# A hybrid encoder layer on one core: another order of the projections in the heads phase

## The reference

```
h = rms_norm(x, norm_mix);  u, q, zf, zb, iv, g = split(h @ w_in)          # six parts of 512
k = (1-lb) * sigmoid(-z);  f = 1-k                                         # forward (zf) and backward (zb)
o = gated recurrence of (silu(q), k, iv, f), forward + backward, 4 heads of 128
y_rec = rms_norm(o, hgrn_out_norm) * silu(g)                               # over the 128 values of a head
y_fourier = per-group product with w_fnet of real(fft2(u))
x = x + concat(y_fourier, y_rec) @ w_out
x = x + expert_choice_ffn(rms_norm(x, norm_ffn))                           # 16 experts, top-k tokens of each
return rms_norm(x, norm_final)
```

## Time and profile before

| | before |
|---|---|
| time, median of 3 | 3081.16 us (3079.77 to 3086.99) |
| span of the profiled execution | 3080.7 us |
| TensorE busy (matmul) | 2841.2 us, 92% |
| VectorE busy | 1684.3 us, 55% |
| ScalarE busy | 1352.7 us, 44% |
| GpSimd busy | 225.1 us, 7% |
| heads phase | from 52.8 us, its last matmul near 728 us, the next phase's loads from 731.1 us |

### The profile page before, as it was taken

One profiled execution on the slowest core, in us unless ns is written; L12 is line 12 of the kernel. 1 busy time (PEld: TensorE's weight loads), 2 busy tenths in 40 slices (PEclk: granted clock), 3 DMA queues, 4 the chain that ended last, 5 costly groups with the idle time before them and its releaser, 6 DMA issues. The chain is left out here.

```text
span 3080.7 us, 33698 instructions
## 1 busy us (share of the span) xinstructions
PE 2841.2 (92%) x13072; PEld 2310.5 (75%) x13072; DVE 1684.3 (55%) x1861; ACT 1352.7 (44%) x1324; POOL 225.1 (7%) x258
## 2 busy tenths in 40 slices
PE   6998989898899399999999999999999999999992
PEld 5777777787677377777877877877778778778771
DVE  4455555543233755655655566556556555665562
ACT  5233333322243245454554555554545545545442
POOL 2010101010100110000000000000000000000001
PEclk9999999999999599999999999999999999999996
DMA  4000000004732456565665665665656656656645
GB/s 133 14 18 28 18 28 18 28 31 144 242 127 89 154 201 218 219 237 197 232 221 208 238 222 207 226 223 218 231 206 231 223 206 238 225 204 228 211 164 181
DMA packets 66293, 515.08 MB, mean 167 GB/s; under 512 B 7952, under 2 KB 8592, under 8 KB 41648
## 3 DMA queue, kind: packets, MB, share of 16 engines
q1 hardware_dynamic: 47952, 449.41, 40.0%
q0 software_dynamic: 18272, 64.74, 7.2%
HBM read 473.57 MB, written 40.89 MB: 167 GB/s over the span
## 5 line engine op out<-in xcount | busy, mean ns | idle before, releaser
L1325 DVE TENSOR_TENSOR big_lo<-ew_raw,big_hi 128x4096 fp32r<-128x4096 f32 x191 | 845.1, 4425 | 483.3 <-ACT big_hi L1265 483.3
L1265 ACT CAST big_hi<-ew_raw 128x4096 fp32r<-128x4096 f32 x192 | 697.5, 3633 | 104.2 <-PE p_bank L1443 91.5
L1439 PE MATMUL s_bank<-big_hi,x_parts 128*128 128x512 f32 x1024 | 404.8, 395 | 1.4 <-DVE x_parts L1334 1.4
L1443 PE MATMUL p_bank<-big_lo,x_parts 128*128 128x512 f32 x1024 | 399.3, 390 | 0.0
L1441 PE MATMUL s_bank<-big_lo,x_parts 128*128 128x512 f32 x1024 | 399.3, 390 | 0.0
L1440 PE MATMUL s_bank<-big_hi,x_parts 128*128 128x512 f32 x1024 | 399.2, 390 | 0.0
L1442 PE MATMUL p_bank<-big_hi,x_parts 128*128 128x512 f32 x1024 | 398.8, 389 | 0.0
L45 PE MATMUL bank<-big_hi,w_hi 128*128 128x512 f32 x576 | 240.7, 418 | 6.6 <-DMA lb<-in_lb_params 6.3
L47 PE MATMUL bank<-big_hi,w_lo 128*128 128x512 f32 x576 | 229.8, 399 | 0.0
L46 PE MATMUL bank<-big_lo,w_hi 128*128 128x512 f32 x576 | 229.8, 399 | 0.0
L1439 PEld LDWEIGHTS s_bank<-big_hi,x_parts 128*128 128x128 f32 x1024 | 192.5, 188 | 43.0 <-issue 1.6
(11 more groups left out here) (217 smaller groups left out, 3928.1 us busy)
## 6 DMA issues: line engine op xcount, KB each, us to landing
ew_raw<-in_expert_weights SPq DMA_DIRECT2D x192, 2048.0 KB, 7.7
w_raw<-in_w_heads SPq DMA_DIRECT2D x48, 256.0 KB, 2.9
tab<-in_tables POOLq DMA_DIRECT2D x20, 512.0 KB, 5.7
x_in<-in_x SPq DMA_DIRECT2D x12, 512.0 KB, 4.1
raw_d<-mixer_y SPq DMA_DIRECT2D x24, 256.0 KB, 3.4
x_d<-in_x POOLq DMA_DIRECT2D x12, 512.0 KB, 4.8
residual<-x_d POOLq DMA_DIRECT2D x12, 512.0 KB, 2.9
ffn_in<-h_d POOLq DMA_DIRECT2D x12, 512.0 KB, 2.9
```

The costliest lines, as they stand in the source:

```text
L1265: nc.scalar.copy(w_hi[:, c % RING], raw[:, c % RAW]).then_inc(hi_done, 1)
L1325: nc.vector.tensor_tensor(w_lo[:, c % RING], raw[:, c % RAW], w_hi[:, c % RING].bitcast(F32), ALU.subtract).then_inc(lo_done, 1)
L1439: nc.tensor.matmul(s_bank[i][:], operand[:, t, S_HI], hi, start=a, stop=False)
L1443: last = nc.tensor.matmul(p_bank[i][:], operand[:, t, P_BOTH], lo, start=False, stop=b)
```

## The change

The projections become one stream that runs three halves further ahead: the list starts with 13 halves instead of 10, and slots 0 to 7 hold G | Q | Q | ZF | ZF | ZB ZB | V V | G (the first is the second half of the next block's G, the last three are the first halves of the block after that). `vt` stands behind the first half of G instead of directly behind V. The state products `u` of block n-1 move from the end of that block to behind level 0 of block n (those of block 11 stay where they were). Within a slot the halves still come ahead of the recurrence and of the norm. In slot 5 of the blocks n % 3 = 1 the order is ZB ZB, `square`, `ss`; in n % 3 = 0, slot 4 is ZF, `square`, `ss` of part 1, and slot 5 is ZB ZB, `bc` of part 1, `square`, `ss` of part 2. Behind block 11 the list ends with the last `fnet` half, `bc`, `square`, `ss`, `bc`.

`bc` no longer builds diagonal matrices: TensorE takes a column of `rstd`, repeated 128 times, as the stationary operand and the identity as the moving one.

```diff
-        timeline = proj(0, V) + proj(0, G) + [("vt", 0)] + proj(0, Q) + proj(0, ZF) + proj(0, ZB)
-        fnet_halves = [e for g in range(GROUPS) for b in range(NB) for e in proj(NN + b, g)]
-        FNET_FILL = (2, 1, 1, 2, 1, 1, 1, 1)
+        stream = []
+        for n in range(NN):
+            stream += proj(n, V) + [("begin", n, G), ("vt", n), ("proj", n, G)]
+            stream += [e for j in (Q, ZF, ZB) for e in proj(n, j)]
+        stream += [e for g in range(GROUPS) for b in range(NB) for e in proj(NN + b, g)]
 
         def take_halves(count):
-            return [fnet_halves.pop(0) for _ in range(min(count, len(fnet_halves)))]
-
+            taken = []
+            while stream and (count or stream[0][0] == "vt"):
+                count -= stream[0][0] != "vt"
+                taken.append(stream.pop(0))
+            return taken
+
+        LEAD = 3
+        FILL = (1, 1, 1, 1, 1, 2, 2, 1)
+        timeline = take_halves(2 * NJ + LEAD)
...
             for s in range(8):
                 if n < NN:
                     timeline.append(("level", n, s))
-                timeline += fill[s]
+                if s == 0 and n >= 1:
+                    timeline += [("u", n - 1, 0), ("u", n - 1, 1)]
+                if n < NN:
+                    timeline += take_halves(FILL[s])
+                for ev in fill[s]:
+                    timeline += take_halves(ev[1]) if ev[0] == "fill" else [ev]
             if n < NN:
-                timeline += [("intra", n), ("kt", n, 0), ("kt", n, 1), ("u", n, 0), ("u", n, 1)]
-        timeline += fnet_halves
+                timeline += [("intra", n), ("kt", n, 0), ("kt", n, 1)]
+        timeline += take_halves(len(stream))
...
-                        k_tok_unused(dve, ev, 1)
-                        step(nc.vector.reciprocal(rstd[:], rms[:]))
-                        for c in range(CH):
-                            last = nc.vector.tensor_scalar(k_tok[:, 1, c], ident[:], rstd[:, c:c + 1], None, ALU.mult)
-                        last.then_inc(diag_ready, 1)
+                        nc.vector.reciprocal(rstd[:], rms[:]).then_inc(rstd_ready, 1)
...
-                            last = nc.tensor.matmul(bank[i][:, c], ones[:], k_tok[:, 1, c], start=(c == 0),
-                                                    stop=(c == CH - 1), skip_group_check=True)
+                            last = nc.tensor.matmul(bank[i][:, c], rstd[:, c:c + 1].to_broadcast([P, P]), ident[:],
+                                                    start=(c == 0), stop=(c == CH - 1), skip_group_check=True)
```

More of the change, by code:

```diff
@@ L220, in heads_phase @@
         ident = sb("ident_b", [P, P])
-        ones = sb("ones", [P, P])
+        ones = sb("ones", [P, 1])
         onorm = sb("onorm", [P, 1])
@@ L239, in heads_phase @@
         NN = HEADS * NB
-        timeline = proj(0, V) + proj(0, G) + [("vt", 0)] + proj(0, Q) + proj(0, ZF) + proj(0, ZB)
-        fnet_halves = [e for g in range(GROUPS) for b in range(NB) for e in proj(NN + b, g)]
-        FNET_FILL = (2, 1, 1, 2, 1, 1, 1, 1)
-        def take_halves(count):
-            return [fnet_halves.pop(0) for _ in range(min(count, len(fnet_halves)))]
+        stream = []
[3 more added lines that the diff above has]
+        stream += [e for g in range(GROUPS) for b in range(NB) for e in proj(NN + b, g)]
+        def take_halves(count):
+            taken = []
[6 more added lines that the diff above has]
+        timeline = take_halves(2 * NJ + LEAD)
         for n in range(NN + 1):
             fill = [[] for _ in range(8)]
[L249 to L257, removed]
             if n >= 1 and n % NB != 2:
@@ L270, in heads_phase @@
                     if n == NN:
-                        fill[i // 2] += take_halves(1 if i else 2)
+                        fill[i // 2] += [("fill", 1 if i else 2)]
                 for b in blocks:
@@ L274, in heads_phase @@
                     last = n == NN
-                    fill[f] += [("square", h, b)] + take_halves(2 * last) + [("ss", h, b)]
-                    fill[f + 1] += take_halves(1 * last) + [("bc", h, b)]
+                    fill[f] += [("square", h, b), ("fill", 2 * last), ("ss", h, b)]
+                    fill[f + 1] += [("fill", 1 * last), ("bc", h, b)]
             for s in range(8):
@@ L329, in heads_phase @@
         squared, weighed = sem("o_squared"), sem("o_weighed")
-        diag_ready = sem("diag_ready")
+        rstd_ready = sem("rstd_ready")
         u_stored = sem("u_stored")
@@ L345, in k_tok_unused @@
             past = timeline[:timeline.index(ev)]
-            for kind in ("u", "ss" if d == 0 else "bc"):
+            for kind in ("u", "ss") if d == 0 else ("u",):
                 users = [e for e in past if e[0] == kind and (kind != "u" or e[2] == d)]
@@ L718, in _ @@
                         for c in range(CH):
-                            last = nc.tensor.matmul(bank[i][:, 0, c:c + 1], k_tok[:, 0, c], ones[:, 0:1], start=(c == 0),
+                            last = nc.tensor.matmul(bank[i][:, 0, c:c + 1], k_tok[:, 0, c], ones[:], start=(c == 0),
                                                     stop=(c == CH - 1), skip_group_check=True)
@@ L722, in _ @@
                     elif kind == "bc":
-                        pe.wait_ge(diag_ready, order["bc"][ev] + 1)
+                        pe.wait_ge(rstd_ready, order["bc"][ev] + 1)
                         for c in range(CH):
-                            last = nc.tensor.matmul(bank[i][:, c], ones[:], k_tok[:, 1, c], start=(c == 0),
-                                                    stop=(c == CH - 1), skip_group_check=True)
+                            last = nc.tensor.matmul(bank[i][:, c], rstd[:, c:c + 1].to_broadcast([P, P]), ident[:],
+                                                    start=(c == 0), stop=(c == CH - 1), skip_group_check=True)
                         last.then_inc(bank_filled[i], 1)
```

## The result

The changed kernel takes 3115.98 us (median of 4 runs, 3107.58 to 3119.09), the kernel before 3082.01 beside it: ratio 1.0105, 95% interval 1.0089 to 1.0121. The forecast was 3103 with a range of 3083 to 3121: the direction and the mechanism were right, the size a third too small.

A forecast was written before the change was run, and what follows sets the result against it. TensorE was taken to bound the heads phase, so only its waits were priced: 64.2 us come, 47.8 go, net +16.4, plus 6 for the clock, giving 3103 us, 8-in-10 range 3083 to 3121.

The forecast's parts named there:

- (a) to (c): Waits that go: vt on V's copy 10.8 us, eleven of u 6.7, block 0's key sum and short key wait 4.0.
- (e): Odds and ends in slot 3, where G stood: 2 us saved.
- (4): Levels wait for keys behind G and Q, 7.5 us more; level 5's 2.14 us wait moves to level 4, same price.
- (d) and (2): bc: all ten old waits go, 24.3 us; three new ones behind ZB, n % 3 = 0, 5.8 each, 17.4.
- (1): inter on the state behind G or Q: ten waits instead of three, 16.1 us, plus 3.9 for three table loads.
- (3): ss directly behind ZB or ZF, waiting for the square: 2.7 us three times, 1.6 otherwise, 14.5 in sum.
- (5): SyncE's queue: late weight loads stop ScalarE's cast, delaying the copy of vt, 0.9 us three times, 2.8.
- (6): Behind the last fnet half, bc, square, ss, bc uncovered: bank wait 1.0 and chain 1.0, 2.0 us.
- The clock: Lower clock behind more long TensorE waits in the heads phase: +6 us, bounds 0 and +14.
- rival B: It cancels: waits of levels and SyncE's queue are swallowed by others, clock falls no oftener; 3087 us, chance 0.21.
- Rival C: Faster: hand-over behind the sigmoid is hidden for inter and ss; 3059 us, chance 0.11.
- rival D: Dearer: repeated column loads slowly, or table switches have the longer price; 3115 to 3121 us, chance 0.08.

The follow-up runs named there:

- e6: Changed kernel with the squares ahead of a slot's halves and the bc of part 1 between the halves of ZB: 3071.80 us, ratio 0.9966.
- e5: Changed kernel with 183 matmuls, results overwritten, put in front of waits of bc, ss and inter: 3097.49 us, ratio 1.0049.
- e4: Changed kernel with the updates of a slot ahead of its halves: 3086.97 us, ratio 1.0022.
- e1: Kernel before with the new bc alone (repeated column of rstd, no diagonals): 3050.33 us, ratio 0.9899.
- e7: Kernel before with the new bc and vt one slot later, behind the first half of G: 3033.72 us, ratio 0.9856.

## Why the prediction came out as it did

It was right in its direction and in nearly all of its places, and two thirds of the size. Its sum counts from start to start, the profile idle time, a difference of 0.16 us for each wait, some 0.6 us in the net. The sizes by its own steps:

- **(a) to (c), waits that go**: nearly as forecast. `vt`, level 0 on the key sum and eleven waits of `u` are gone. `intra`, directly behind `vt`, now waits for its end ten times, 3.0 us in all, where a level had done so for 1.2. The second half of (c) was a misreading: beside the four waits of 2.14 us has not one short wait on keys but four, of 0.27 at the most, in blocks 0, 2, 5 and 8; those of (4) have taken their place. The 2 us of (e) stood on no row, and no run shows them.
- **(d) and (2), bc**: forecast 5.8 us from start to start; measured 5.36 of idle time. In blocks n % 3 = 1 none, as forecast. e6 shows that the cover was the cause.
- **(1), inter**: forecast 2.3 us each and 3.9 for the table loads, 27 us where the ten waits now stand; the profile shows 27.1 of idle time in these ten, in the forecast places, and 2.7 in five short ones, for 0.7 before. Behind a table load the longest is 4.0 and not 3.4: the weight subtraction on GpSimd falls on VectorE's copy of the state, 2.11 us for two (block 4, from 307.00), and 0.36 in block 3, where GpSimd is idle. The longer distance was in no row of before.
- **(3), ss**: forecast 14.5, measured 14.5 of idle time in seven waits, the longest 2.58.
- **(4), levels**: four waits of 2.19 us stand at level 4, behind Q, in place of the four of 2.14 at level 5. The other eight, behind the delays of slots 0 and 2 in blocks 0, 2, 5 and 8, come to 6.4 us, or 7.7 from start to start, for the 7.5 forecast.
- **(5), SyncE's queue**: ScalarE's casts waited three times for the load, 13.7 us in all. Only a little of it reaches TensorE, 1.9 us in three waits on the copy of `vt`, for the 2.8 forecast. Timeline of block 3 in the changed kernel:

```profile
292.27 6.95 SPq L69 DMA_DIRECT2D w_raw<-in_w_heads  x4
...
295.67 1.25 ACT L73 CAST w_hi<-w_raw 128x512 fp32r<-128x512 f32 x2 [4.80 <-DMA w_raw<-in_w_heads]
296.82 0.58 ACT L464 COPY v_tok<-bank 128x512 f32<-128x512 f32 x1
297.46 1.09 PE L700 MATMUL bank<-ident_b,kq 128*128 128x128 f32 x8 [0.84 <-ACT v_tok L464]
```

- **(6), tail**: 0.85 us for the bank and 0.66 for the chain, for the 2.0 forecast.
- **The repeated operand**: nothing, as taken (190 ns for a load, 275 for a matmul; before 192 and 275).
- **The clock: the term that was most mis-sized.** I took +6 with bounds of 0 and +14. Busy time grew by 14.3 us, just beyond the upper bound, and by e5 all that the lower clock costs behind the filled waits is 18 to 20 us. The proportion in the working was nearly right: 27 us withheld with 48 us of long waits, and 29 us more of such waits, give 16 (I wrote 10 or more). I then went down to 6 because the lower clock had followed only half of the long waits; but the 27 us are what was withheld with only half of them followed, so that discount was counted twice.
- **The sum of the waits**: +23.0 us of idle time for +16.4. `inter` came out 3.7 us larger, `ss` 1.1, `intra` (1.8) and the missing gain of (e) (2.0) weren't in the sum, and (2), (5) and (6) came out 1.4 smaller. That is 7.2 us for a gap of 6.6 or, with the 0.6 above, 6.0; each figure is good to some tenths.

By blocks the forecast had some 62 us for n % 3 = 0 and 52 for n % 3 = 1. Blocks 3, 6 and 9 take 66.9 to 68.8 us from first level to first level, and block 1 takes 56.5: in block 3 TensorE's busy time alone grew by 4.8 us (50.8 to 55.6, clock 0.85 for 0.94), in block 1 by 4.4 (43.6 to 48.0, clock 0.91 for 1.00).

The rival B rested on waits that swallow each other. e4 and e6 show them separate: each repair took out its own rows and left the other's. Rival C would have needed `inter` and `ss` to wait little; they wait 44 us. The half of rival D that rests on the repeated operand is refuted by e1. The drain that the Trainium skill gives behind a table load ("ScalarE: Activation LUTs", "What ACT_TABLE_LOAD costs") doesn't show here either: the table load ends at 273.26 and the sigmoid starts at 273.27. The 3115 that this figure gave is near the measured time, but the time was in the clock, not there.

## What to carry to other kernels

When work is moved to give one wait more cover, list for every event what now stands directly in front of it; on in-order engines an event inherits the whole chain of whatever precedes it, here up to 5.4 us for a reciprocal of 0.17. Issue the side operations (update, square, reciprocal) ahead of the large block of matmuls that is to cover them, and what consumes them behind it: the same lead with this order is 82 us faster. The lead itself won nothing: e7, in the old order with the new `bc` and late `vt`, reaches the same 3034 us. Expect a TensorE wait to cost more than its length, since the matmuls behind it may run at the lower clock: in this change 23.0 us of idle time came with 14.3 us of busy time. It is no fixed price; in e7 waits of 2.1 to 2.7 us stood eight times in the phase and the clock stayed at 1.00. And time the parts of a change apart, since one of these was worth 29 us alone and hardly anything in the whole.

## What I had not expected of the hardware

The clock moves the time nearly as much as the waits do. e1 removed 16 us of waits and won 12 more in busy time; the phase of e7 had a mean clock of 1.00 with 41.2 us of idle time in it, while the kernel before, with 65.7 us of idle time, took 612.6 - 589.1 = 23.5 us more of busy time for the same number of instructions. Matmuls that compute nothing, put into waits of 1.7 to 5.4 us, brought 18.5 us. And beside a GpSimd subtraction of 128x512 VectorE's products of that size took 2.1 and 2.6 times as long (1.45 and 1.78 us for 0.69, e4), so its place in the order is part of the schedule too.
